# Interleaving the first unit's gathering with its gate products, and reading the expert order behind the first refill

## The reference

```python
h = x
n = rms_norm(h, norm1_g)
p = n @ w_in                                  # queries, keys, values of two head groups
h = h + concat(rms_norm(global_attention), rms_norm(window_attention)) @ w_o
h = h + hier_moe(rms_norm(h, norm2_g), ...)   # below
out = rms_norm(h, final_g)

def hier_moe(x, ...):                         # 4 groups of 8 experts, D = 1024, F = 512
    group = argmax(x @ w_group + b_group)     # top-1 group, then top-2 experts in it
    combine = group share * renormalised top-2 weights
    for each of the 32 experts:
        y += (silu(x @ w_gate[e]) * (x @ w_up[e]) * combine[e]) @ w_down[e]
```

## Time and profile before

| | us |
|---|---|
| median of 3 runs | 575.41 (575.11 to 576.01) |
| the profiled execution, its own time | 575.66 |
| its span | 573.8 |
| PE busy | 451.8 (79%) |
| DVE busy | 117.3 (20%) |
| ACT busy | 62.5 (11%) |
| transfers, 218.72 MB | mean 381 GB/s |

### The profile page before, as it was taken

The page is one execution under the profiler, slowest core; times in us unless marked ns, Lnnn a source line. Parts: engine busy times, 40 slices in busy tenths (PEclk is TensorE's granted clock), DMA queues, the critical chain, the costliest instruction groups (busy, mean ns, idle before and its releaser), DMA issues.

```text
span 573.8 us, 6223 instructions
## 1 busy us (share of the span) xinstructions
PE 451.8 (79%) x2544; PEld 199.6 (35%) x2544; DVE 117.3 (20%) x282; ACT 62.5 (11%) x127; POOL 28.2 (5%) x58
## 2 busy tenths in 40 slices
PE   8999989999999994395999955765665765577565
PEld 3446767564535341041353511231113111322111
DVE  1017664252101212000212120012001200120204
ACT  1114233222010100000101000000000000000002
POOL 0052200040000000000000000000000000000001
PEclk9999999999999997887999987689868886897897
DMA  7989990855999999999999999999999999999982
GB/s 277 405 320 429 425 354 0 330 183 185 423 402 431 410 427 429 429 424 433 424 430 423 431 426 429 426 428 427 429 426 426 433 423 434 422 429 426 420 342 75
DMA packets 25342, 218.72 MB, mean 381 GB/s; under 512 B 5304, under 2 KB 6584, under 8 KB 13280
## 3 DMA queue, kind: packets, MB, share of 16 engines
q1 hardware_dynamic: 21072, 215.36, 89.9%
q10 hardware_dynamic: 4240, 2.94, 1.7%
HBM read 217.23 MB, written 1.06 MB: 380 GB/s over the span
## 4 chain that ended last, share of the span: by engine, by line
PE 54%; DMA 40%; SPq 2%; DVE 2%; issue 1%; POOL 0%; ACT 0%; POOLq 0%; DVEq 0%; ACTq 0%
PE bank L1266 20%; DMA ring<-in_w_gate_dram 14%; DMA ring<-in_w_down_dram 14%; DMA ring<-in_w_up_dram 12%; PE bank L1281 8%; PE bank L1056 7%; PE bank L1125 4%; PE bank L1317 3%; PE bank L1237 3%; PE bank L1115 2%; SPq L400 2%; PE bank L1104 1%; PE bank L1093 1%; PE bank L1037 1%; PE bank L1048 1%
## 5 line engine op out<-in xcount | busy, mean ns | idle before, releaser
L1266 PE MATMUL bank<-ring,region_x 128*32 128x512 f32 (+1 forms) x1024 | 162.3, 683 | 79.8 <-DMA ring<-in_w_up_dram 47.0
L1266 PEld LDWEIGHTS bank<-ring,region_x 128*32 128x32 f32 (+1 forms) x1024 | 47.3, 130 | 186.7 <-issue 186.7
L1281 PE MATMUL bank<-ring,region_q 128*32 128x512 f32 (+1 forms) x512 | 81.7, 684 | 29.7 <-DMA ring<-in_w_down_dram 28.1
L928 DVE TENSOR_TENSOR h<-h,bank 128x512 f32<-128x512 f32 x40 | 27.5, 688 | 116.5 <-PE bank L1317 116.5
L1281 PEld LDWEIGHTS bank<-ring,region_q 128*32 128x32 f32 (+1 forms) x512 | 23.4, 129 | 79.9 <-issue 73.2
L1056 PE MATMUL bank<-ring,region_x 128*128 128x512 f32 x96 | 42.2, 594 | 0.0
L1237 PE MATMUL bank<-region_q,region_t 128*128 128x128 f32 x320 | 39.8, 278 | 0.3 <-DVE region_q L901 0.3
L1237 PEld LDWEIGHTS bank<-region_q,region_t 128*128 128x128 f32 x320 | 37.3, 192 | 7.8 <-issue 7.8
L1317 PE MATMUL bank<-region_x,region_q 128*128 128x512 f32 x80 | 38.9, 619 | 0.0
L922 DVE TENSOR_TENSOR region_q<-region_q,bank 128x512 f32<-128x512 f32 x10 | 6.9, 688 | 119.4 <-PE bank L1266 119.4
L1125 PE MATMUL bank<-ring,region_q 128*128 128x512 f32 x64 | 28.9, 597 | 0.0
(11 more groups left out here) (183 smaller groups left out, 246.4 us busy)
## 6 DMA issues: line engine op xcount, KB each, us to landing
ring<-in_w_up_dram SPq DMA_DIRECT2D x31, 2048.0 KB, 33.8
ring<-in_w_gate_dram SPq DMA_DIRECT2D x28, 2048.0 KB, 32.5
ring<-in_w_down_dram SPq DMA_DIRECT2D x27, 2048.0 KB, 34.9
ring<-in_w_in_dram SPq DMA_DIRECT2D x8, 768.0 KB, 12.5
ring<-in_w_down_dram SPq DMA_DIRECT2D x12, 512.0 KB, 18.0
ring<-in_w_o_dram SPq DMA_DIRECT2D x2, 2048.0 KB, 11.9
ring<-in_w_gate_dram SPq DMA_DIRECT2D x8, 512.0 KB, 7.2
ring<-in_w_gate_dram SPq DMA_DIRECT2D x4, 1024.0 KB, 9.8
```

Source lines behind the costliest of these rows:

```text
L928: dve.tensor_tensor(part, part, ps[SC0 + k % 2][:], ALU.add).then_inc(sc_free, 1)
L1266: last = pe.matmul(ps[bank][rows, :], xgT[:, c, rows], slots[fill_slot(f + a)][:, c * F:(c + 1) * F], start=(c == 0), stop=(c == KC - 1))
L1281: last = pe.matmul(ps[GD0 + half][rows, :], hT[:, c, rows], slots[fill_slot(f + a)][:, c * D + 512 * half:c * D + 512 * half + 512], start ...
```

## The change

SP: the first quarter of the down matrix is issued as soon as the first gate quarter is free; the wait for `order_ready` and the reading of the list come behind it, ahead of the first quarter of unit 2's gate.

PE: unit 0's gather and gate products are interleaved. Behind gather half 0 come chunks 4 and 5 of the gather, gate chunks 0 and 1 (which need half 0 alone, so `xg_act`), the order product, gate chunks 2 and 3, chunks 6 and 7 of the gather, the picks and ranks turned, and gate chunks 4 to 7 behind `xg_dve`. The programs of DVE, ACT and GpSimd are unchanged.

```diff
             down_slot, gate_slot = slots[fill_slot(down_fill)], slots[fill_slot(gate_fill)]
-            sp.wait_ge(order_ready, 1)
-            experts = order_of(2)
             for c in range(PIECES):
...
                 sp.dma_start(down_slot[:, cols], down_e[3][:, cols]).then_inc(first_pieces_in if c < PIECES - 1 else slot_in[fill_slot(down_fill)], 16)
+                if c == 0:
+                    sp.wait_ge(order_ready, 1)
+                    experts = order_of(2)
                 sp.dma_start(gate_slot[:, cols], gate_e[bass.ds(experts[0], 1), :, cols].rearrange("a p n -> (a p) n")).then_inc(
...
+            def gather_chunks(b, chunks):
+                for c in chunks:
+                    for t in range(TT):
+                        last = pe.matmul(ps[GD0 + b][:, c * P:(c + 1) * P], hn[:, t, 4 * b + c, :], pick[:, t, :],
+                                         start=(t == 0), stop=(t == TT - 1))
+                return last
...
+            def first_gate(chunks):
+                for c in chunks:
+                    for a in range(2):
+                        rows = expert_rows(2, a)
+                        last = pe.matmul(ps[GATE][rows, :], xgT[:, c, rows], slots[fill_slot(a)][:, c * F:(c + 1) * F],
+                                         start=(c == 0), stop=(c == KC - 1))
+                    if c % 2 == 1:
+                        last.then_inc(gate_done if c == KC - 1 else gate_pieces, 1)
+
             gather_half(0, 0)
-            gather_half(0, 1)
+            gather_chunks(1, range(0, 2))
+            pe.wait_ge(xg_act, 1)
+            for a in range(2):
+                landed(fill_at(0, 0, a))
+            first_gate(range(0, 2))
             pe.wait_ge(places_ready, 1)
             pe.matmul(ps[SC1][0:1, 128:128 + EXPERTS], expert_col, place_hot[0:EXPERTS], start=True, stop=True).then_inc(ordered, 1)
+            first_gate(range(2, 4))
+            gather_chunks(1, range(2, 4)).then_inc(gathered, 1)
             turn_picks(0)
             for k in range(2 * TT):
                 last = pe.transpose(ps[SC0][0:EXPERTS, k * P:(k + 1) * P], (rank1, weight)[k // TT][:, k % TT, :], ident)
             last.then_inc(ranks_turned, 1)
-            products(0, 2, fill_at(0, 0, 0), GATE, gate_done, gate_pieces)
+            pe.wait_ge(xg_dve, 1)
+            first_gate(range(4, KC))
             pe.wait_ge(ranks_cut, 1)
```

More of the change, by code:

```diff
@@ L1234, in gather_half @@
                     pe.wait_ge(y_ready, 2 * i - 3 + b)
[L1235 to L1239, removed]
+                gather_chunks(b, range(4)).then_inc(gathered, 1)
             def turn_picks(i):
```

## The result

The changed kernel takes 576.81 us (median of 20 runs), the kernel before 575.68 in the 20 runs beside it. The ratio is 1.0031, 95% interval 1.0016 to 1.0045: **slower by 0.9 to 2.6 us**. The 1.0031 isn't the ratio of the two medians, which lie 1.13 us apart. The profiled execution of the changed kernel took 577.17, its span is 575.3, 1.5 us longer than before's 573.8.

The account below looks back on a forecast made before the run. The transfer stream was taken to bound the kernel: restart +1.7 us, less 1.0 absorbed by two dips, gives +0.7, from a median of 575.41 to 576.1 us; the 8-in-10 range was 575.1 to 577.6.

Parts of the forecast that it names:

- The bound: Weight transfers: the end is set by the stream's start after the router, bytes over rate, and stretches below its rate.
- PE's order, +0.44: Unit 0's interleaved gather and gate on PE: gate ends at 139.25 instead of 138.81, +0.44 us, bounds 0 to 0.8.
- The late order, 4.0 us: DVE's cast to `expert_at`, behind the copy of the later gather half, ends at 135.66, 4.0 us later.
- SP's position: SP's issues: first down quarter at 131.76, 2.36 us earlier; first gate quarter at about 138.2, after four register loads.
- The stream after the restart, +1.7: Seven quarters restarting from an empty queue: stream 1.7 us later at 144, bounds +0.6 to +2.9.
- rival 3: Slower: the restart pays the full ramp again, short 4 KB rows; +1.9 (577.3) to +2.9 (578.3); chance 0.27 with rival 1's upper tail.
- The dips give back 1.0: Stream dips at 166 to 170 and 196 to 200, 0.5 us each, absorb up to 1.0 us of lateness.
- The end, +0.7: End of the kernel: 1.7 - 1.0 = 0.7 us later, over a floor of 0.44 from PE's later releases.
- Rival 4: Faster, by more than 1.15 us, below 574.3; even an order in time would lose nearly all at 166; chance 0.03.

Follow-up runs that it names:

- e7: Kernel before, with unit 1's two gate slots refilled in quarters as PE uses them instead of whole; ratio 0.9984 (0.9957 to 1.0012).
- e2: Kernel before with only SP's change: the order is read behind the first down quarter; ratio 1.0011 (0.9990 to 1.0032).
- e3: Changed kernel, with DVE casting the order ahead of its copy of gathered half 1; ratio 1.0002 (0.9984 to 1.0020).
- e1: Changed kernel's PE order with SP as before, waiting for the order ahead of the first quarter; against the kernel before, ratio 1.0042 (1.0026 to 1.0059).
- e4: As e3, with SP reading one register of the order ahead of the first gate quarter and three behind the eight quarters; ratio 1.0010 (0.9991 to 1.0028).
- e11: Changed kernel, with the order read behind the second down quarter instead of the first; ratio 1.0028 (1.0011 to 1.0045).
- e9: As e8, with unit 2's four gate slots also refilled in quarters as PE uses them; ratio 1.0020 (0.9996 to 1.0044).
- e8: Kernel before, order product inside gather half 1, cast first, one register first, next order read ahead, unit 1's gate slots in quarters; ratio 0.9984 (0.9961 to 1.0006).
- e12: The changed kernel itself measured again, beside e11; ratio 1.0037 (1.0017 to 1.0057).
- e5: Changed kernel, with unit 2's first gate matrix in two 1 MB halves instead of four quarters; one execution only, 576.92 us.

## Why the prediction was right or wrong

- **The bound** (a transfer stream, paced by PE's releases until 200 us and at 427 GB/s from there on): the rate held, 426 or 427 over 200 to 540 us in every run here. The pacing is shown for the dip of 166 (e7) and for the late stream (e2); that no run lifted the mean over 73 us above 360 is not explained.
- **PE's order, +0.44**: measured 0.54, near by size and partly by luck. From the gather's start to its end 7.90 us (7.83 expected), 0.76 from there to the gate's last part (0.88), and 3.65 for that part (3.51). The second gather part cost 0.15 more for standing behind gate products (1.10 against 0.95; 0.18 expected). But the gate's three parts took 1.87 + 1.87 + 3.65 = 7.39 us against 7.02 in one piece, and for these 0.37 I had nothing; what I had for the order product (0.19) and for the stall behind DVE's copy (0.2) hardly came (0.15 against 0.14; 0.76 against 0.81 before). What the Trainium skill says of drains ("TensorEngine Tiling (Array Packing)", "Key Properties"), charged at entries too, would have been 0.8. The 0.54 lies between, and whether the 0.37 is paid on entering the gate products or on leaving them, these rows don't tell.
- **The late order, 4.0 us, and SP's position**: cast at 135.72 (135.49 expected; 0.16 of it is the gather's start), first down quarter 132.01 (131.76), first gate quarter 138.50 (138.2). e3 shows the cause of the late refill by moving one instruction, e1 that SP's half of the change saves a part of it, not the whole.
- **The stream after the restart, +1.7: the term that was mis-sized.** It was 2.4. The seven quarters ran at 297 GB/s in 139 to 146. With the first bytes 0.9 us behind the issue, at 139.4, as I had counted before, that is 2.08 MB, 4.9 us at 427, in 6.6 us: a loss of 1.7. I had taken the loss of two restarts with 2 MB transfers, 0.7 and 1.1 us; the eight quarters of before had lost 2.3. So rival 3's mechanism was there by three quarters, just where I had put its border. For its reason (short rows) there is little: halves gave 306.
- **The dips give back 1.0**: they gave 2.4 - 1.4 = 1.0 us, and both went away. This part held, also in e2, where 0.8 us of delay vanished.
- **The end, +0.7**: +1.5 by the span and +0.9 to +2.6 by the times, between the forecast (0.5 to 1.15) and rival 3 (1.9). 576.81 lies in the range of 575.1 to 577.6, 0.7 above the 576.1; some 0.3 of that is that the kernel before had a median of 575.68 beside it and not 575.41. I gave slower by over 0.2% a chance of 0.27 and no measurable change 0.70; the ratio is 1.0031 with an interval of 1.0016 to 1.0045. So a loss is measured, and it is by luck more than by the odds I gave that the range holds it. Had I taken the upper restart cost, the quarters' own 2.3 us and not that of 2 MB transfers, the forecast would have been 1.9 and the sign clear.
- **Rival 4** (an order in time gains nearly nothing) is what e3 and e4 show, with the place corrected: the queue runs dry at 155 first.

## What to carry to other kernels

When a step is moved, ask what stands behind it in another engine's program: here the order product came where it should, and its tiny cast waited 3.6 us behind a copy that needed the part that had been moved away. An operation whose consumer is an issuing queue belongs ahead of the copies beside it. A wait for a value that comes late belongs behind the issues that don't need it (by the bytes of e1 and e11; their times don't show it). Where the value is there in time, that can be wrong: e2 had the order early, read it behind the first quarter all the same, and started the rest of the stream later than before, by the register loads. And before a transfer stream is started earlier, look for the next place where it waits for a release: in e4 an earlier start won nothing beyond it, while a later start costs all that exceeds the slack.

## What the runs showed of the hardware

A restart of the transfer stream from an empty queue ran below its rate for some 5 us, 297 GB/s over 7 us against 427, with 512 KB quarters and nearly the same (306) with 1 MB halves; the two restarts with whole 2 MB transfers lost 0.7 and 1.1 us. What makes the difference is open.

In the profiled execution of e9 PE's granted clock fell to the lower of its two levels (0.50, 1.2 of 2.4 GHz) during the gather. The third column from the end is the granted clock:

```profile
122.00:125.00 3.00, 1.82 (x6) 0.63 (x4) 2.79 (x20) 0.59 (x3) 0.00 (x0) 1.00 0.39 152
125.00:127.00 2.00, 1.73 (x16) 1.63 (x17) 1.55 (x11) 0.00 (x0) 0.00 (x0) 1.00 0.70 240
127.00:129.00 2.00, 2.00 (x15) 2.00 (x14) 1.66 (x10) 0.00 (x0) 0.00 (x0) 0.72 0.01 4
129.00:131.00 2.00, 2.00 (x11) 1.86 (x9) 0.00 (x0) 0.60 (x1) 0.00 (x0) 0.50 0.00 0
131.00:133.00 2.00, 2.00 (x17) 1.58 (x16) 0.71 (x2) 0.00 (x0) 0.00 (x0) 0.93 0.00 0
```

The sixteen gather records took 2.72 us there, 2.02 in e8, and the first refill slid by a us and a half counted from the gather's start. So e9's 350 is this and not its edit. PE had been idle in the router before it fell (1.82 busy of 3.00 us), but that doesn't decide it: e12 had 1.87 and e1, e7 and e11 had 2.15 or 2.16 in the same 3 us, and their clock stayed at 1.00. In five other executions (the changed kernel, e2, e4, e5, e8) the clock fell earlier, in the router itself, to a mean of 0.77 to 0.84 over 119 to 122 and 0.59 to 0.66 over 122 to 125 us, and was back at 1.00 ahead of the gather. What sets the moment is open.
